# Four merges per layer moved from VectorE to GpSimd in the mixer of a hybrid decoder trunk

## What is computed

```python
y_d = jnp.einsum('bsnc,ncd->bsnd', ys, w_branch[layer])       # three branches, 512 -> 1024
gates = jax.nn.sigmoid(gate_logits...reshape(B, S, 3, 1024))
merged = jnp.sum(gates * y_d, axis=2)
x = x + merged @ w_out[layer]
```

## Time and profile before

| what | value |
|---|---|
| median of 3 runs (lowest, highest) | 1057.05 us (1057.03, 1057.7) |
| span of the profiled execution, first to last instruction | 1054.9 us |
| TensorE busy | 1040.3 us, 99% |
| VectorE busy | 835.6 us, 79% |
| ScalarE busy | 678.2 us, 64% |
| GpSimd busy | 139.5 us, 13% |
| mean granted TensorE clock | 0.998 |

### The profile page before, as it was taken

One profiled execution on the slowest core, in us unless ns is written; L12 is line 12 of the kernel. 1 busy time (PEld: TensorE's weight loads), 2 busy tenths in 40 slices (PEclk: granted clock), 3 DMA queues, 4 the chain that ended last, 5 costly groups with the idle time before them and its releaser, 6 DMA issues.

```text
span 1054.9 us, 15494 instructions
## 1 busy us (share of the span) xinstructions
PE 1040.3 (99%) x5669; PEld 848.5 (80%) x5669; DVE 835.6 (79%) x1172; ACT 678.2 (64%) x971; POOL 139.5 (13%) x166
## 2 busy tenths in 40 slices
PE   8999999999999999999999999999999999999997
PEld 7988888888888888999887878777777777677775
DVE  6879776988666766687967797898898888889895
ACT  7776746556443534676665655877777777777773
POOL 5004330001100000000613000450101010101011
PEclk9999999999999999999999999999999999999999
DMA  9543534467456446363344448799899999999993
GB/s 287 196 160 112 172 129 158 165 228 271 146 208 234 165 140 201 100 216 122 129 160 149 171 140 298 256 385 349 314 359 389 374 327 394 377 387 364 391 371 88
DMA packets 131282, 252.74 MB, mean 240 GB/s; under 512 B 6606, under 2 KB 56868, under 8 KB 131204
## 3 DMA queue, kind: packets, MB, share of 16 engines
q1 hardware_dynamic: 129444, 245.93, 66.0%
q0 software_dynamic: 1296, 4.20, 1.9%
q10 hardware_dynamic: 464, 1.58, 0.4%
HBM read 247.49 MB, written 4.19 MB: 239 GB/s over the span
## 4 chain that ended last, share of the span: by engine, by line
PE 92%; DVE 4%; issue 1%; ACT 1%; DMA 1%; POOL 0%; SPq 0%; DVEq 0%; POOLq 0%; ACTq 0%
PE PS L805 29%; PE PS L1346 12%; PE PS L1348 11%; PE PS L1347 11%; PE PS L1210 8%; PE PS L1211 4%; PE PS L1159 2%; PE PS L1157 2%; PE PS L1158 2%; PE PS L829 2%; PE PS L1017 1%; DVE m_lo L2193 1%; PE PS L1301 1%; DVE scr L2499 1%; DVE big L2491 1%
## 5 line engine op out<-in xcount | busy, mean ns | idle before, releaser
L498 DVE TENSOR_TENSOR w_lo<-ring,w_hi 128x1536 fp32r<-128x1536 f32 (+1 forms) x191 | 306.1, 1618 | 81.0 <-ACT w_hi L489 80.3
L489 ACT ACTIVATE w_hi<-ring 128x1536 fp32r<-128x1536 f32 (+1 forms) x192 | 261.8, 1369 | 99.8 <-PE PS L1211 47.8
L1633 ACT ACTIVATE m_hi<-ring 128x512 fp32r<-128x512 f32 (+2 forms) x256 | 157.5, 631 | 120.0 <-PE PS L805 118.1
L2193 DVE TENSOR_TENSOR m_lo<-ring,m_hi 128x512 fp32r<-128x512 f32 (+2 forms) x256 | 181.9, 742 | 58.7 <-ACT m_hi L1633 56.6
L805 PE MATMUL PS<-m_hi,h_both 128*128 128x512 f32 (+3 forms) x640 | 178.6, 366 | 1.2 <-DVE m_lo L2193 1.2
L805 PEld LDWEIGHTS PS<-m_hi,h_both 128*128 128x128 f32 x640 | 113.1, 188 | 20.2 <-DVE m_lo L2193 2.9
L1210 PE MATMUL PS<-h_both,w_hi 128*128 128x512 f32 x352 | 124.4, 399 | 0.0
L805 PE MATMUL PS<-m_lo,h_both 128*128 128x512 f32 (+3 forms) x320 | 115.1, 360 | 0.0
L1346 PE MATMUL PS<-w_hi,hTe 128*96 128x512 f32 (+1 forms) x288 | 108.9, 378 | 0.0
L1348 PE MATMUL PS<-w_lo,hTe 128*96 128x512 f32 (+1 forms) x288 | 108.3, 376 | 0.0
L1347 PE MATMUL PS<-w_hi,hTe 128*96 128x512 f32 (+1 forms) x288 | 107.8, 374 | 0.0
(11 more groups left out here) (378 smaller groups left out, 1965.5 us busy)
## 6 DMA issues: line engine op xcount, KB each, us to landing
ring<-in_w_in_dram SPq DMA_DIRECT2D x39, 1024.0 KB, 5.0
ring<-in_w_exp_gate_dram SPq DMA_DIRECT2D x48, 768.0 KB, 8.3
ring<-in_w_exp_up_dram SPq DMA_DIRECT2D x48, 768.0 KB, 7.8
ring<-in_w_exp_down_dram SPq DMA_DIRECT2D x24, 1536.0 KB, 9.1
ring<-in_w_branch_dram SPq DMA_DIRECT2D x12, 1024.0 KB, 5.1
ring<-in_w_ffn_gate_dram SPq DMA_DIRECT2D x12, 768.0 KB, 5.3
ring<-in_w_ffn_up_dram SPq DMA_DIRECT2D x12, 768.0 KB, 6.0
ring<-in_w_ffn_down_dram SPq DMA_DIRECT2D x6, 1536.0 KB, 6.4
```

Source lines behind the costliest of these rows:

```text
L489: act.activation(split_parts(u, j)[0], ring[:, i % NSLOT, w0:w0 + words], ACT.Copy)\
L498: dve.tensor_tensor(lo, ring[:, (j // 2) % NSLOT, w0:w0 + words], hi.bitcast(F32), SUB).then_inc(sem(f"lo_ready{b}"), 1)
L1633: act.activation(hi, raw, ACT.Copy).then_inc(sem("m_hi_ready"), 1)
L2193: dve.tensor_tensor(lo, raw, hi.bitcast(F32), SUB).then_inc(sem("m_lo_ready"), 1)
```

## The change

The four merges of branch 2 in each layer leave VectorE's list and are appended to GpSimd's list for the layer, behind its last `qkd` product. GpSimd waits for the semaphore that `gated(2, m)` raises (that of the freed PSUM bank) and raises a new semaphore, `two_merged`. The merges of branch 1 stay on VectorE and wait for `two_merged` in addition. VectorE's remaining operations are put in another order: all four pieces of `br10` are split one after the other, and the third piece of `br11` is split ahead of `gated(1, 0)` without a merge between.

To have a semaphore free for it, semaphores that were each raised once by one engine are put together into three that count (`routing_known`, `tables_built`, `scalar_set`); who waits for what, and where, stays as it was.

```diff
+ROUTING_KNOWN = {"logit_gap": 1, "totals_read": 2, "top_inverse": 3, "passes_known": 4}
+TABLES_BUILT = {"angles": 1, "windows": 2, "router_ready": 3}
+SCALAR_SET = {"first_gain": 1, "gains_ready": 2, "rope_tables": 3, "top_exp": 4}
...
@@ GpSimd, mixer
                 for v in range(3, LEVELS + 1):
                     decayed(v)
+                for m in range(2 * TT):
+                    hf, a = divmod(m, 2)
+                    _, _, free, n = use(L, f"b2{hf}{a}")
+                    pool.wait_ge(free, n + 1)
+                    dst = merged[:, a, hf * 512:(hf + 1) * 512]
+                    pool.tensor_tensor(dst, dst, gates[:, 4 + hf, a, :], ADD).then_inc(sem("two_merged"), 1)
...
@@ VectorE, mixer
                     freed(L, f"b{n}{hf}{a}")
-                    ins = dve.tensor_tensor(dst, dst, g, ADD)
-                    if n == 2:
-                        step(ins)
-                    else:
-                        ins.then_inc(sem("merged"), 1)
+                    dve.wait_ge(sem("two_merged"), 4 * L + m + 1)
+                    dve.tensor_tensor(dst, dst, g, ADD).then_inc(sem("merged"), 1)
...
                 yt_low(0), yt_low(1)
-                split(L, "br10", [0]), merge(2, 0), split(L, "br10", [1]), merge(2, 1), split(L, "br10", [2, 3])
-                gated(2, 2), split(L, "br11", [0]), gated(2, 3), split(L, "br11", [1]), merge(2, 2)
-                split(L, "br11", [2]), merge(2, 3)
+                split(L, "br10"), gated(2, 2), split(L, "br11", [0]), gated(2, 3), split(L, "br11", [1, 2])
                 gated(1, 0), merge(1, 0), gated(1, 1), merge(1, 1)
                 split(L, "br11", [3])
```

More of the change, by code:

```diff
@@ L721, in _ @@
                 expert_loads(eg, eu, ed, e, e)
[L723 removed]
+            sp.wait_ge(sem("routing_known"), ROUTING_KNOWN["passes_known"])
             npass = sp.value_load(npi[0:1, 0:1], min_val=1, max_val=PASSES)
@@ L1434, in _ @@
             one_pass(0)
-            pe.wait_ge(sem("passes_known"), 1)
+            pe.wait_ge(sem("routing_known"), ROUTING_KNOWN["passes_known"])
             npass = pe.value_load(npi[0:1, 0:1], min_val=1, max_val=PASSES)
@@ L1515, in _ @@
                 if L == 0:
-                    pool.wait_ge(sem("windows"), 1)
+                    pool.wait_ge(sem("tables_built"), TABLES_BUILT["windows"])
                 W = PADW + T
@@ L1755, in mixer @@
                 if L == 0:
-                    act.wait_ge(sem("angles"), 1)
-                    act.activation(cs[:, :, :], ang[:, 1:3, :], ACT.Sin).then_inc(sem("rope_tables"), 1)
+                    act.wait_ge(sem("tables_built"), TABLES_BUILT["angles"])
+                    act.activation(cs[:, :, :], ang[:, 1:3, :], ACT.Sin).then_inc(sem("scalar_set"), 1)
                 def out_gate(i):
@@ L1785, in mixer @@
                 if L == 0:
-                    act.wait_ge(sem("gains_ready"), 1)
+                    act.wait_ge(sem("scalar_set"), SCALAR_SET["gains_ready"])
                 for x in QUADS:
@@ L2033, in _ @@
             one_pass(0)
-            act.wait_ge(sem("passes_known"), 1)
+            act.wait_ge(sem("routing_known"), ROUTING_KNOWN["passes_known"])
             npass = act.value_load(npi[0:1, 0:1], min_val=1, max_val=PASSES)
@@ L2086, in angles @@
                     else:
-                        ins.then_inc(sem("angles"), 1)
+                        ins.then_inc(sem("tables_built"), 1)
             def window_table():
@@ L2106, in rope_factors @@
             def rope_factors():
-                dve.wait_ge(sem("rope_tables"), 1)
+                dve.wait_ge(sem("scalar_set"), SCALAR_SET["rope_tables"])
                 dve.wait_ge(sem("grope_in"), 16 * 2 * DEPTH)
@@ L2356, in mixer @@
                 if L == 0:
-                    dve.wait_ge(sem("gains_ready"), 1)
+                    dve.wait_ge(sem("scalar_set"), SCALAR_SET["gains_ready"])
                     dve.wait_ge(sem("router_in"), 16)
@@ L2750, in top_inverse @@
             def top_inverse():
-                dve.wait_ge(sem("top_exp"), 1)
+                dve.wait_ge(sem("scalar_set"), SCALAR_SET["top_exp"])
                 step(dve.tensor_scalar(rsm[:, 4:6], rsm[:, 2:4], 1.0, None, ADD))
-                dve.reciprocal(rsm[:, 4:6], rsm[:, 4:6]).then_inc(sem("top_inverse"), 1)
+                dve.reciprocal(rsm[:, 4:6], rsm[:, 4:6]).then_inc(sem("routing_known"), 1)
             def passes():
-                dve.wait_ge(sem("totals_read"), 1)
+                dve.wait_ge(sem("routing_known"), ROUTING_KNOWN["totals_read"])
                 step(dve.tensor_scalar(rsm[:, 9:10], rsm[:, 8:9], float(CAP), 1.0, ALU.is_gt, ADD))
@@ L2801, in _ @@
             one_pass(0)
-            dve.wait_ge(sem("passes_known"), 1)
+            dve.wait_ge(sem("routing_known"), ROUTING_KNOWN["passes_known"])
             npass = dve.value_load(npi[0:1, 0:1], min_val=1, max_val=PASSES)
```

32 lines of the change are left out of this document (16 added, 16 removed).

## The result

The changed kernel takes 1058.46 us (median of 21 runs) beside 1057.05 us for the kernel before (21 runs): ratio 1.0012, with an interval of 1.0007 to 1.0018. That is slower by 1.4 us where +0.5 was forecast: inside the 0.2% that was called no change, and 0.06 us above the upper end of the range (1058.4).

The account below looks back on a forecast made before the run. TensorE bounds the kernel, waiting once per layer for VectorE's last merge; turns with GpSimd delay gated(1,0) by 0.25 us per layer, +0.5 in two layers, so 1057.05 becomes 1057.55 us, range 1055.8 to 1058.4.

Parts of the forecast that it names:

- What bounds the place: TensorE's second merged transposes wait for VectorE's list ending at merge(1,1); at most 0.66 us per layer to gain.
- What the removal would bring alone: With four merges off VectorE and no other effect, gated(1,0) starts at 204.87, 0.79 us earlier.
- Turns between splits and merges; gated products unhindered: VectorE splits and GpSimd merges, reading SBUF, wait for each other's end; gated products read PSUM and aren't held.
- The plain gain, in which GpSimd gets no turn until VectorE pauses: Rival: GpSimd doesn't hold the splits; the full 0.66 per layer is won, 1055.7 us; chance 0.1.
- the cast of the earlier trace: GpSimd cast of 16 elements in the expert stage, 6.10 us while VectorE runs without pause; cited for the plain gain.
- GpSimd first by 0.05 at `br11` piece 0: GpSimd's third merge starts at 201.56, the split of piece 0 could at 201.61; the split then ends at 203.30.
- The rival with VectorE first: VectorE's split of br11 piece 0 starts first: gated(1,0) 0.48 earlier, 1056.1 us; chance 0.2 for one layer or both.
- The length of a turn: A GpSimd merge takes 1.2 us finding the port free, or ends 0.93 after the split it waited for.
- The bound of 1.41: Upper bound for one GpSimd merge, from 530 elements including waiting; rival at this bound: +0.8, 1058.35 us; longer merges' chance 0.1.
- The first transposes stay: TensorE's transposes of the first 128 tokens keep their start at 207.48, merge(1,0) being ready by 207.47.
- the sign the prediction named for longer merges: A first transpose that waits too, or waits for GpSimd, would mean merges longer than assumed.
- The first two merges, the added wait, the triangular table: First two GpSimd merges harmless (a br10 split waits 0.3); two_merged wait met long before; moved table costs nothing.

Follow-up runs that it names:

- e3: Changed kernel with GpSimd's adds replaced by only raising the semaphore (branch 2 missing from the sum): 1055.79 us beside 1056.89 before.
- e5: Changed kernel with each GpSimd add replaced by zeroing 128x1024 of a buffer of its own (branch 2 missing from the sum): 1055.79 us beside 1056.98 before.
- e2: Changed kernel with each GpSimd merge cut into two operations of 256 columns: 1056.31 us beside 1056.89 before.
- e7: Changed kernel with six empty GpSimd instructions ahead of the third merge, so VectorE's split starts first: 1056.95 us beside 1056.98 before.
- e10: Changed kernel measured once more, unaltered, with a profile of its own: 1058.35 us beside 1056.94 before.
- e6: Changed kernel with only merges (2,0) and (2,1) on GpSimd; (2,2) and (2,3) back on VectorE at their old places: 1057.01 us beside 1056.98 before.
- e1: Changed kernel with joined semaphores kept, but all merges back on VectorE in the old order, without the added wait: 1057.29 us beside 1056.89 before.
- e4: Kernel before with merge(2,3) moved behind merged_low(1), everything still on VectorE: 1056.06 us beside 1056.89 before.

## Why the prediction was right in kind and too small in size

- *What bounds the place.* Right: the end of VectorE's list at `merge(1,1)`, worth 0.66 per layer. e3 and e5 won 0.65 to 0.70, and TensorE waited for a merge nowhere else.
- *What the removal would bring alone.* Right to 0.01: `gated(1,0)` at 204.87 (e3).
- *Turns between splits and merges; gated products unhindered.* Right. e2, e3, e5 and e7 change one thing each (length, presence, reading, order), and the splits follow each time. The signs came too: 0.70 us of idle ahead of the second transposes, 1.29 and 1.67 for the third and fourth merge, 1.79 for a held split.
- *The plain gain, in which GpSimd gets no turn until VectorE pauses.* Not here: in the changed kernel GpSimd's fourth merge got its turn between the splits of pieces 1 and 2, which follow one another without a pause. But the cast of the earlier trace rows did wait, and the row of VectorE beside it in the kernel before shows that starting first didn't help it:

```profile
687.20 1.75 DVE L498 TENSOR_TENSOR w_lo_last<-ring,w_hi_last 128x1536 fp32r<-128x1536 f32 x1
```

  The cast starts at 687.12, 0.08 ahead of this operation, which has two inputs in SBUF as a split has, and holds it not at all: one of the same size takes 1.76 at 232.63, where GpSimd has nothing to do. So that GpSimd wins by starting 0.05 ahead is what the merges did, not a rule of this trace; what decides between the two cases no run tested.
- *GpSimd first by 0.05 at `br11` piece 0.* Right in both layers (202.02 against 202.07, 615.39 against 615.45), and again in e10. The rival with VectorE first would have cost nothing, as e7 shows (-0.04 and -0.10); its forecast gain of 0.48 per layer was too large for the reason of the next point.
- *The length of a turn.* Mis-sized, and this is where the number failed. A merge that finds the port free takes 1.29 us (estimated 1.2), and one that had to wait ends 1.14 behind the split (estimated 0.93 from the earlier trace rows). On the old clock: the third merge ends at 202.84 instead of 202.76, the split of piece 0 at 203.39 instead of 203.30, the fourth merge at 205.74 instead of 205.44, `gated(1,0)` at 206.21 instead of 205.91. The two errors, 0.09 and 0.21, add to the 0.30 by which the forecast of +0.25 falls short of the measured +0.55. The 0.93 came from an operation of another shape, 530 elements in the pooling sums; that it would hold for a merge I assumed, as I did the 0.2 to 0.3 of start that waiting hides (it hid 0.15). The number of elements isn't the reason, since a merge has fewer, 512. The pooling sums cost less for each element. In the trace of before the add of 807 ends 1.39 us behind its split, 0.46 more than the one of 530, or 1.65 ns for each further element; from a half merge, 0.60 behind its split in e2, to a whole one it is some 2.1 ns. Why they differ no run tells. The bound of 1.41, meant to include a wait, held for the third merge but not for the fourth, which took 1.67 with its wait. The range allowed 0.2 more on each of two turns in a layer, 0.4, and the turns needed 0.30 of it; what carried the median past the end of the range is the remainder below.
- *The first transposes stay.* Wrong by 0.28 for the same reason: they start at 208.23 - 0.47 = 207.76, where they stood at 207.48. That is the sign the prediction named for longer merges. It costs nothing more, since the second ones wait for later merges anyway.
- *The first two merges, the added wait, the triangular table.* Right: no cost of the first two (e6, e3); the second layer, which has the table, loses no more than the first (+0.51 against +0.54). The joined semaphores: none in the stage (e1).

What stays open is a remainder of some 0.36 us: the mixers account for +1.05, the medians say +1.41, so the longer turns explain 0.55 of the 0.9 by which the forecast change of 0.5 fell short. The interval of the ratio (+0.7 to +1.9 us) holds both. It isn't peculiar to the change: in all ten experiments the median lies above the distances, by 0.05 (e6) to 0.59 (e2), and by 0.35 in e4, which has neither the joined semaphores nor the new one (-0.83 beside -1.18). In the two profiles it stands ahead of the mixers: the changed kernel's span is 1.5 us longer, of which 1.05 is the mixers and 0.47 the start of the program up to the `qk` transposes. But the start varies: in the profile of e10, taken on the shortest of its runs (1057.79), it is 0.31 shorter than before's. No run told whether the remainder is more than the measurement's spread.

## What to carry to other kernels

Before a two-input operation goes to GpSimd to relieve VectorE, look at which two-input VectorE operations lie beside it and what waits for them; the held time shows as busy, so the page looks unchanged. If the deadline is VectorE's own list, move the work past the deadline on the same engine first (e4: one line, nearly the whole gain). If it has to be GpSimd, keep it where no one waits for the held operation (e6), or cut it into short pieces (e2), and price the turn from an operation of the same size and the same kind of inputs.

## What the runs showed of the hardware that I had not expected

- A GpSimd operation that has waited for its turn saves little of its own time: 1.14 us behind the split's end in the changed kernel and 1.15 in e7 (the split at 202.90 ends at 204.00, the pair at 205.15), where a fresh one takes 1.29.
- After a GpSimd add the held split ends 0.55 behind it, close to the rate of 0.60 at which VectorE's operations follow one another, whether it was held by a whole merge or a half.
- The start of the program varies more than the change is worth: the `qk` transposes of the first layer start between 192.68 (e10) and 194.15 (e4), so two profiles can't be compared by their spans or by raw starts.
